# Sliding-window attention mixers: the key range moves into a bias block reloaded from DRAM, the first out slot's low weights move ahead of values and softmax, and all scores take the 256-key tile first

## The reference

```python
A_WINDOW = 128
dist = pad + qi - kj
in_band = (dist >= 0) & (dist < window)
bias = rel_table[rel_bucket(dist)]                  # by head
s = einsum("bqgrd,bkgd->bgrqk", q_n, k_n) * scale + bias
p = masked_softmax(s, in_band & (start - pad + kj >= 0), sink)
o = einsum("bgrqk,bkgd->bqgrd", p, v_n)
...
for i in range(4):                                  # layers of the second block
    x = x + 0.5 * rms_norm(swiglu_2(rms_norm(x, g[0]), ...), g[1])
    m = (A, B, C, A)[i](rms_norm(x, g[2]))
    x = x + rms_norm(m, g[3])
    x = x + 0.5 * rms_norm(swiglu_2(rms_norm(x, g[4]), ...), g[5])
```

## Time and profile before

| what | value |
|---|---|
| median of 3 runs | 2696.5 us (2692.08 to 2701.61) |
| span of the profiled execution | 2693.9 us |
| PE busy | 2601.8 us, 97% of the span |
| DVE busy | 1815.6 us, 67% |
| ACT busy | 1467.9 us, 54% |
| POOL busy | 173.1 us, 6% |
| DMA | 465.44 MB, mean 173 GB/s |
| first A stage | starts at 903.9 us, next stage at 993.6 us |
| second A stage | starts at 2409.7 us, next stage at 2500.7 us |

### The profile page before, as it was taken

How to read it: one execution, slowest core, us unless ns; L and a number is a source line. 1 busy time by engine, 2 the same in 40 slices (tenths; PEclk the granted TensorE clock), 3 DMA queues, 4 the chain that set the end, 5 groups by cost and what they waited for, 6 DMA issues and landing times.

```text
span 2693.9 us, 44003 instructions
## 1 busy us (share of the span) xinstructions
PE 2601.8 (97%) x15456; PEld 2255.8 (84%) x15456; DVE 1815.6 (67%) x2565; ACT 1467.9 (54%) x2363; POOL 173.1 (6%) x253
## 2 busy tenths in 40 slices
PE   7999998999999989999989999999999999998999
PEld 6888887888888868888888688888888888887887
DVE  5766668666766666676676666676657667666766
ACT  4645447455555564565555655555555555555654
POOL 0010001000000030000001200000110000002000
PEclk9999999999999999999999999999999999999999
DMA  4458744477566436666654266666446665653664
GB/s 150 145 164 231 210 129 142 156 226 212 172 193 190 133 121 208 191 184 193 187 176 153 70 199 191 177 192 191 141 149 183 196 202 168 192 157 121 180 189 146
DMA packets 581774, 465.44 MB, mean 173 GB/s; under 512 B 19524, under 2 KB 542372, under 8 KB 581156
## 3 DMA queue, kind: packets, MB, share of 16 engines
q1 hardware_dynamic: 579300, 456.10, 56.3%
q0 software_dynamic: 1632, 7.37, 1.1%
q10 hardware_dynamic: 736, 0.56, 0.1%
HBM read 460.76 MB, written 4.25 MB: 173 GB/s over the span
## 4 chain that ended last, share of the span: by engine, by line
PE 83%; DVE 7%; ACT 5%; issue 2%; DVEq 2%; DMA 1%; POOL 1%; SPq 0%; ACTq 0%; POOLq 0%
PE acc L783 19%; PE gu L750 14%; PE tp L750 13%; PE tp L757 7%; PE gu L757 7%; PE acc L816 3%; DVE lo_a L452 3%; ACT hi_a L440 1%; PE acc L1454 1%; PE acc L1456 1%; PE acc L1455 1%; PE gu L701 1%; PE gu L1412 1%; PE tp L1327 1%; PE gu L1413 1%
## 5 line engine op out<-in xcount | busy, mean ns | idle before, releaser
L452 DVE TENSOR_TENSOR lo_a<-raw_a,hi_a 128x2048 fp32r<-128x2048 f32 (+1 forms) x313 | 711.1, 2272 | 357.4 <-ACT hi_a L440 356.1
L440 ACT ACTIVATE hi_a<-raw_a 128x2048 fp32r<-128x2048 f32 (+1 forms) x313 | 591.5, 1890 | 119.0 <-PE acc L1456 27.4
L750 PE MATMUL tp<-xT,hi_a 128*128 128x512 f32 x1600 | 398.4, 391 | 0.0
L750 PE MATMUL gu<-xT,hi_a 128*128 128x512 f32 x1600 | 397.9, 391 | 0.0
L750 PEld LDWEIGHTS gu<-xT,hi_a 128*128 128x128 f32 x1600 | 294.0, 188 | 56.9
L750 PEld LDWEIGHTS tp<-xT,hi_a 128*128 128x128 f32 x1600 | 293.4, 188 | 56.4
L783 PE MATMUL acc<-hi_b,h_hi 128*128 128x512 f32 x760 | 298.6, 393 | 1.6 <-issue 1.1
L783 PE MATMUL acc<-lo_b,h_hi 128*128 128x512 f32 x760 | 298.0, 392 | 0.0
L783 PE MATMUL acc<-hi_b,h_lo 128*128 128x512 f32 x760 | 295.7, 389 | 0.0
L464 DVE TENSOR_TENSOR lo_b<-raw_b,hi_b 128x1024 fp32r<-128x1024 f32 x210 | 255.9, 1219 | 0.0
L842 ACT ACTIVATE arena<-arena 128x256 f32<-128x256 f32 x200 | 83.6, 418 | 282.0 <-DVE arena L905 282.0
(11 more groups left out here) (329 smaller groups left out, 4109.4 us busy)
## 6 DMA issues: line engine op xcount, KB each, us to landing
raw_a<-in_ffn_w_in SPq DMA_DIRECT2D x352, 512.0 KB, 5.7
raw_b<-in_ffn_w_out SPq DMA_DIRECT2D x176, 512.0 KB, 3.6
raw_a<-in_w_in SPq DMA_DIRECT2D x52, 512.0 KB, 4.7
raw_a<-in_w_gate SPq DMA_DIRECT2D x44, 512.0 KB, 5.5
raw_a<-in_w_up SPq DMA_DIRECT2D x44, 512.0 KB, 6.7
raw_b<-in_w_down SPq DMA_DIRECT2D x44, 512.0 KB, 4.4
raw_a<-in_w_out SPq DMA_DIRECT2D x24, 512.0 KB, 4.2
raw_a<-in_c_w_in SPq DMA_DIRECT2D x24, 512.0 KB, 4.5
```

Source lines behind the costliest of these rows:

```text
L440: nc.scalar.activation(a_view(hi_a, par)[:, :, 0:width], a_view(raw_a, par)[:, :, 0:width], ACT.Copy).then_inc(a_hi, 1)
L452: nc.vector.tensor_tensor(a_view(lo_a, par)[:, :, 0:width], a_view(raw_a, par)[:, :, 0:width], a_view(hi_a, par)[:, :, 0:width].bitcast(F3 ...
L750: nc.tensor.matmul(banks[:, e, :], w_hi[:, kt, e * P:(e + 1) * P], xT[:, :, kt, :], start=(kt == 0), stop=False)
```

## The change

Four edits go together.

1. The window's constants and their addition in every A softmax go. A row of the bias in DRAM grows from 384 to 640 columns: 128 of -1e30 and a copy of the columns of distances 127 to 0 follow. Read from offset 511, the middle block (columns 128 to 256) has the window in it; read from 127, as before, it has not.
2. The middle block in `bias` is the windowed one for the first A stage, and is reloaded twice: plain in the feed-forward stage behind the first A, windowed in the one ahead of the second A. SP's loop over tiles is cut after tile 5 for it. DVE waits for the landing ahead of the mixers.
3. `behind` ends one slot earlier, so the first out slot's low split stands ahead of values and softmax.
4. The scores of every mixer (hybrid, A, B, C) take the token tile with 256 keys first.

```diff
-                      ("dilated", 384), ("window", 128), ("invf", 1), ("pad", 1), ("cmpbias", 32),
+                      ("dilated", 384), ("invf", 1), ("pad", 1), ("cmpbias", 32),
...
-        scratch = nc.dram_tensor("bias_rows", (NH, 384), F32).ap()
-        spread = nc.dram_tensor("bias_spread", (NH, P, 384), F32).ap()
+        scratch = nc.dram_tensor("bias_rows", (NH, 640), F32).ap()
+        spread = nc.dram_tensor("bias_spread", (NH, P, 640), F32).ap()
...
-            cuts = (1, 3, 5, 7, FT // 2) if early else (1, FT // 2)
+            plain_back = stages[s.k - 1].kind == "A" and s.k + 1 < len(stages)
+            window_again = s.k + 1 < len(stages) and stages[s.k + 1].kind == "A" and stages[s.k + 1].j == 1
+            cuts = (1, 3, 5, 7, FT // 2) if early else (1, 3, FT // 2) if plain_back or window_again else (1, FT // 2)
             for lo, hi in zip(cuts, cuts[1:]):
-                if lo > 1:
-                    bias_sync(sp, s, (lo - 3) // 2)
+                if lo > 1 and early:
+                    bias_sync(sp, s, (lo - 3) // 2, windowed=lo == 5)
+                elif lo > 1:
+                    bias_sync(sp, s, 1, windowed=window_again)
...
-            if s.kind == "A":
-                nc.vector.tensor_tensor(prob[:, :, 128:256], prob[:, :, 128:256],
-                                        C("window").unsqueeze(1).broadcast_to([P, 2, P]), ALU.add)
-                dve.drain()
...
-            for t in range(NT):
+            for t in (1, 0):
                 for hh in range(2):
...
             pre_dve(dve, s)
+            dve.wait_ge(scratch_in, 48 if s.kind == "A" and s.j == 0 else 64 if s.kind == "C" else 80)
             dve.wait_ge(rb_ready, s.pre + 1)
...
-                    behind = s.kind == "A" and i < n_proj
+                    behind = s.kind == "A" and i < n_proj - 1
...
-            src = bass.AP(spread.tensor, (255, 127, 255)[k], [[383, P], [P * 384, NH], [1, P]])
+            src = bass.AP(spread.tensor, 511 if windowed else (255, 127, 255)[k], [[639, P], [P * 640, NH], [1, P]])
...
-            nc.vector.tensor_tensor(bias_row[0:NH, :], tp[0:NH, 1, 0:384], C("future", NH), ALU.add).then_inc(bias_row_ready, 1)
+            nc.vector.memset(bias_row[0:NH, 384:640 - A_WINDOW], NEG)
+            nc.vector.tensor_tensor(bias_row[0:NH, 0:384], tp[0:NH, 1, 0:384], C("future", NH), ALU.add)
+            dve.drain()
+            nc.vector.tensor_copy(bias_row[0:NH, 640 - A_WINDOW:640], bias_row[0:NH, 256 - A_WINDOW:256]).then_inc(bias_row_ready, 1)
```

More of the change, by code:

```diff
@@ L107, in constants @@
     put("dilated", np.concatenate(blocks, axis=1))
-    put("window", np.where(P + r[:, None] - r[None, :] < A_WINDOW, 0.0, NEG))
     f = (np.float32(ROPE_THETA) ** (-np.arange(0, ROPE_DIM, 2, dtype=np.float32) / np.float32(ROPE_DIM)))
@@ L296, in build_block @@
         rows = ar(0, 512).rearrange("p (k c) -> p k c", k=4)
-        posb = ar(4480, 256)
+        posb = ar(4736, 256)
         setup_const = ar(11264, CONST_COLS - KEPT_COLS)
         setup_t = ar(15360, 1536).rearrange("p (k c) -> p k c", k=6)
-        bias_row = ar(4096, 384)
+        bias_row = ar(4096, 640)
         ssx, rstdx, nrstdx, eps_y, ssxg = sm(2), sm(2), sm(2), sm(2), sm(2)
@@ L1802, in b_dve @@
             nc.vector.memset(kcd, 0.0)
+            dve.wait_ge(scratch_in, 64)
             dve.wait_ge(rb_ready, s.pre + 1)
@@ L2366, in post_pool, with bias_sync @@
                 nc.gpsimd.tensor_tensor(rstdy[:, t:t + 1], msy[:, t:t + 1], mhalf[:, 0:1], ALU.pow).then_inc(rstdy_ready, 1)
-        def bias_sync(sp, s, k):
+        def bias_sync(sp, s, k, windowed=False):
             for t in range(NT):
@@ L2508, in _ @@
                         pool.wait_ge(a_lo, s.a0 + 3 + h)
-                        src = bass.AP(scratch.tensor, h * 384, [[384, 1], [0, P], [1, 384]])
+                        src = bass.AP(scratch.tensor, h * 640, [[640, 1], [0, P], [1, 640]])
                         pool.dma_start(spread[h:h + 1], src).then_inc(spread_out, 16)
```

## The result

The changed kernel takes 2679.9 us (median of 4 runs, 2678.28 to 2681.72), the kernel before 2699.1 (4 runs, 2692.08 to 2703.55; one run more than when the prediction was made, and its median 2.6 us higher). The ratio is 0.9933 with a 95% interval of 0.9920 to 0.9947, 0.7% less. Run twice more beside other kernels it gave 2678.3 and 2679.7 us, with ratios of 0.9924 and 0.9925. The profiled spans are 2693.9 us before and 2679.9 after, 14.0 us less.

What follows compares the result with a forecast made beforehand. TensorE (PE) is 83% of the chain, so its waits and lower clock in the A stages count. Per A stage 4.5 + 1.25 = 5.75, twice 11.5, clock 4.06, start 0.3: 15.9 off 2696.5, 2681 us; range 2673 to 2690.

Steps and rivals of the forecast that it cites:

- waits ahead of the first out product: A stages, units 0 to 3: PE's waits of 0.73, 0.42 and 0.49 us fall to 0.23, 0 and 0.
- first out product, earlier by: A stages: with the low split in DVE's idle time, it starts at 950.25 instead of 954.75, 4.5 us gained.
- wait left there, its releaser: First out product: PE still waits 0.7 us, released by softmax 4 instead of the low split L452.
- clock behind it, first and second A: Behind the first out product the granted clock no longer falls: 1.40 and 2.66 us gained, 4.06 together.
- tail: A stages, unit 5's scores to PE's last wait: three softmaxes save 1.5, unit 7's returns 0.25, so 1.25 us gained.
- last wait for POOL: End of an A stage: sign of a right forecast, PE's last wait for POOL is near 0.6 us.
- start of the program: Program start: constants lose 64 KB, 0.3 us taken off.
- score order: 48 units issue the wide tile first: same eight passes, 0 gained, bounds 5.0 us either way.
- reloads: Two more 1 MB bias reloads ahead of tile 6 in feed-forward stages: hidden, cost 0, bound 1.8 us.
- Rival 1: A stages: clock still falls behind the waits left; gain 11.8 instead of 15.9, 2685 us; chance 0.14.
- rival 4: First out slot: late high half makes L452 hold the softmax; gain only 5.6, 2691 us; chance 0.06.
- the other order: Rival 2's case, POOL starting before L452: split late by up to 1.6 us, 3.2 in both stages, 2684; rival's chance 0.09.

Runs made afterwards that it cites:

- Edit 3 alone: The kernel before with only the first out slot's low split moved ahead of values and softmax, window addition kept; 2690.8 us against 2699.6 (ratio 0.9971).

## Why the prediction was right, step by step

The forecast was 2681 us and the time is 2679.9; the forecast gain of 15.9 us compares with 14.0 by the two first spans, 14.4 to 16.0 by the A stages of all profiles, and 19.2 by the medians. That the two times lie 1 us apart is in part luck: the forecast was taken off a median of 2696.5 that one more run raised to 2699.1, and the gain that it named is 3.3 us short of the one by the medians. It is borne out by the A stages and by its steps:

| step | forecast | measured |
|---|---|---|
| waits ahead of the first out product | 0.23, 0, 0 | 0.24, 0, 0 |
| first out product, earlier by | 4.5 in each | 4.77 in the first; 3.34 in the second, 4.76 in its third profile |
| wait left there, its releaser | 0.7, the softmax | 0.50 and 0.51, the softmax (L1154) |
| clock behind it, first and second A | 1.40 and 2.66 | 1.44 and 2.67 |
| tail | 1.25 in each | 1.20 and 1.15 |
| last wait for POOL | near 0.6 | 0.84 |
| start of the program | 0.3 | 0.1 here, nothing over the repeats |
| score order | 0 | 0.14 |
| reloads | 0 | 0.0, and 0.0 at three times the bytes |

**The waits.** The walk along DVE's order held within 0.4 us. The 0.27 by which the first out product beat the forecast came along DVE, whose softmax releases it: counted from the start of the stage, the split started 0.2 us ahead of the walk, and unit 4's softmax 0.4, since unit 1's values followed the split with no wait; that softmax then took 0.1 longer. A wait of PE cost somewhat more than its idle time: removing 0.42 moved the product behind it by 0.49, removing 0.49 by 0.65 and removing 0.24 by 0.41.

**The clock.** Behind a wait of 3.79 it fell in 4 of 4 A stages, behind 2.79 in 2 of 2, behind 0.50 in none of 12 (the changed kernel three times, and the three versions of it that leave DVE's order in A alone). That is what the forecast took from the rows at 3.79 and 1.59. Rival 1 fell, and with a first out product 4.77 us earlier so did rival 4.

**POOL and the split.** The split started 0.16 us ahead of POOL, and POOL took 3.57, as forecast. The price that I put on the other order, up to 1.6 us a stage, was wrong: the split was held 0.13 us, by the one POOL instruction that was running. The rule that I quoted, from the Trainium skill, page SBUF — State Buffer, section SBUF: two separate sides, speaks of a lock for one instruction, and the trace agrees with it (617 undisturbed, then 3087); I had applied it to the pair. Edit 3 alone shows what I did not see: where DVE has less room, POOL's held unit is itself what PE waits for, 0.56 and 0.95 us.

**The start.** The 0.3 us for 64 KB less constants was not there: PE's first stage opens at 13.3 and 13.6 us in the two profiles of before, at 13.2, 13.4 and 13.5 in the three of after. The first hybrid stage was 1.08 shorter in this pair of profiles, but the kernel before had 166.44 in its repeat, so that is no effect of the change.

**What stays open** is 3 to 5 us between the medians' 19.2 and the A stages' 14.4 to 16.0. A mean granted clock of 0.992 or more had 15 of the 40 runs of the kernel before that were taken beside the experiments, and 13 of the 14 of the changed kernel; their medians are 2695.7 and 2678.9, 16.8 us apart. So most of the rest lies in the executions of lower mean clock, which the changed kernel had less often (1 of 14; its versions without reloads and with six, of the same order in A, had 3 of 12). The falls in the A stages lower the mean by 10.2 x 0.5 / 2694 = 0.002, so some of the shift is their own; whether the change also makes falls in other stages rarer was not settled, since no profile of the kernel before caught such an execution. One place to look is C: all three profiles with the window's addition (two of the kernel before, one of edit 3 alone) have the fall behind C's opening wait and a C of 122.4 to 122.5 us, against 121.06 in two of three of the changed kernel.

## What to carry to other kernels

When an engine that feeds the critical one is idle ahead of an instruction whose input is late, put into that gap the work that is needed later, and walk along its order to see what is next: here the softmax came 0.5 us behind PE, not 0. Count a wait of several us on TensorE with the clock behind it: a quarter of the forecast gain was the clock, and it came. And release a consumer by the instruction that frees what it needs (the copy out of the accumulators), not by the last one of the step.

## What the hardware showed

The same program loses several us more or less to the lower clock by chance. Two executions of the changed kernel have spans of 2684.6 and 2673.7 us, and the difference of 10.9 stands almost wholly in four places: the two hybrid stages, B, and the second A stage's start (1.4). By stretch, the hybrid stages and B of the second profile, then of the third:

```profile
13.40:181.90 168.50, 155.52 (x1058) 139.73 (x1059) 121.32 (x170) 95.39 (x176) 14.70 (x19) 0.97 0.46 149
368.70:533.30 164.60, 153.44 (x1058) 138.01 (x1057) 115.48 (x155) 88.51 (x169) 13.05 (x18) 0.95 0.43 136
1365.20:1538.00 172.80, 155.69 (x1139) 133.73 (x1137) 112.03 (x187) 98.13 (x228) 29.63 (x40) 0.95 0.40 125
```

```profile
13.50:179.60 166.10, 153.81 (x1059) 138.18 (x1060) 121.32 (x170) 95.39 (x176) 14.72 (x19) 0.97 0.47 151
366.40:527.60 161.20, 149.85 (x1057) 135.06 (x1056) 115.35 (x155) 88.47 (x169) 13.07 (x18) 0.98 0.44 139
1359.70:1528.40 168.70, 152.66 (x1139) 131.73 (x1137) 111.91 (x187) 98.56 (x228) 29.68 (x40) 0.97 0.41 127
```

DVE, ACT and POOL are busy for the same time to 0.1 or, in B, 0.5 us; only the busy times of PE and its weight loads (the first two columns) and the length differ. So a difference of 2 or 3 us in this kernel is read from the stage that was changed, not from the span.

Behind waits of middle length the fall is not fixed either. Behind the opening wait of 1.77 us the second A stage had it in 4 of 14 profiles, C in 6 and the first A stage in none. Two waits of 0.56 and 1.06 us close together had it, 0.95 and 1.06 in the same execution had not, and 1.08 and 1.44 had it in none of 4.
